# Value product of a hybrid attention step: P tiles stationary and 129 columns of V streamed, output turned once per head pair, five low parts on GpSimd

## The chip, the cores and the metric

The kernel runs on one core of one Trainium2 chip. The metric is the device time of one launch in microseconds. TensorE (PE) does the matrix products, VectorE (DVE), ScalarE (ACT) and GpSimd (POOL) the elementwise work, SyncE (SP) issues the DMAs. PEld is TensorE's weight load, which runs beside PE.

## The reference

Four layers run one after the other over 1024 latent and 256 context tokens (1280 queries) of width 1024. Their mixers are multi-head latent attention (MLA, layers 0 and 3), grouped-query attention (GQA, layer 1) and banded attention with a sink logit (SWA, layer 2). Each has 16 heads with values 64 wide. Latent queries see 512 cached and all 1024 latent keys (in SWA only those within 128 tokens), context queries see the 256 context keys. The part that the change touches is, per head:

```python
s = jnp.einsum('bqhgd,bkhd->bhgqk', qb, k) * scale
p = jax.nn.softmax(s, axis=-1)                     # SWA: one more column, the sink
o = jnp.einsum('bhgqk,bkhd->bqhgd', p, v)
out = (o.reshape(B, T, BRANCH) * jax.nn.silu(gate)) @ w_out
```

## The kernel before

Every f32 operand of a product is split into two f16 parts, high and low, and a product is the sum of high·high, high·low and low·high. `attention` handles one layer. It takes the heads in pairs (`NB` = 8 pairs, `body(i, first, last)`); each head is cut into steps. A step is a pair of key blocks of 128 against 512 queries (1024 score columns): 13 steps a head in MLA and GQA (queries 0 to 511, 512 to 1023, and one step for the 256 context queries), 9 in SWA. The three groups of queries are called units 0, 1 and 2. In the MLA layers the pairs between the first and the last run in a hardware loop; the other two layers are written out.

In step p the engines do this, in program order on each queue:

- PE (L2184) computes transposed scores (keys x queries) of step p into one of two score banks, then one or two "max entries" of the next head (L1931, scores again with the queries on the partitions, of which only the row maximum is used), then the value product of step p-2 (L2151, L2153, L2155), then the rest of the entries. A "turn" entry (L1961) transposes the negated row maxima, which ACT then writes as one more row of Q, so that the exponent comes out shifted.
- ACT computes the exponential twice, once as f32 (`p_f`, L2238) and once as f16 (`p_hi`, L2242).
- DVE subtracts them into `p_lo` (L2305), except in the steps of the list `pooled` (5, 7, 10), which POOL does (L2371). DVE also reduces the max entries (L1992).

The value product has V as the stationary operand: 64 value columns beside 64 columns of ones (so that rows 64 to 127 of the result are the softmax denominator), and P streams 512 columns at a time, in three products: `V` with `p_hi`, `VL` with `p_hi`, `V` with `p_lo`. The result is already transposed (values x queries). Its two banks `OB` are used in turn. At the end of a unit ACT makes the reciprocal of the denominator as Ln and Exp of 64 rows (L2258, L2260), DVE multiplies (L2285, `o_f`), POOL multiplies with the gate and splits the result into `H` (L2353, L2357, L2359), 64 rows at a time. In SWA the sink is added to the denominator by one more product (L2158) over three rows of Q.

`make_values` lays out V ahead of the first pair, and the entries share two banks `MB`. What sets the order is this program order and the semaphores alone; there is no scheduler.

Of the kernel before, what the change touches and what calls it, by code (L numbers as in the profile page):

```python
# [23 lines left out]
ALU = mybir.AluOpType  # L24
# [62 lines left out]
class Program:  # L87
    def __init__(self, nc, I, O):
# [10 lines left out]
        self.blk = sb("block_ones", [P, P], F32)  # L99
        self.c16 = sb("const_f16", [P, 5, P], F16)  # L100
# [75 lines left out]
    def start(self, nxt, CK, cache):  # L176
# [31 lines left out]
        consts = [(self.par[:], I["par"]), (cf[:], I["cf"]), (self.ones[:], I["ones"]), (self.blk[:], I["blk"])]  # L208
# [1468 lines left out]
    def attention(self, kind, Q, K, ada_layer, nxt, make_values, v_home=None):  # L1677
# [9 lines left out]
        wide = 3 * P + KD * 32  # L1687
        if v_home is None:
            V = sb("v_hi_ones", [P, 2, NKT, P], F16)
            VL = sb("v_lo_zeros", [P, 2, NKT, P], F16)  # L1690
        else:
            flat = v_home[:].rearrange("p s k n -> p (s k n)")
            V, VL = [flat[:, n * 2 * NKT * P:(n + 1) * 2 * NKT * P].rearrange("p (b t c) -> p b t c", b=2, c=P)
                     for n in range(2)]
        mx = None if swa else sb("max_parts", [P, 2, 4, 3], F32)
        m4 = sb("max_rows", [P, 2, 4], F32)
        turned = 3 if swa else 1
        negm = sb("neg_max", [P, 2, 4, turned], F16)
# [6 lines left out]
        if swa:  # L1705
            sink = self.par[:, self.par.shape[1] - 16:]
            es32 = sb("exp_sink", [P, 2, 4], F32)
            sink_raw = sb("sink_raw", [P, HEADS], F32)

        ident, negi, mask_above, mask_below, sink_ones = [self.c16[:, j] for j in range(5)]  # L1710

        SB, MB, OB = [bank[0], bank[1]], [bank[2][:, 0], bank[2][:, 1]], [bank[3][:, 0], bank[3][:, 1]]
# [52 lines left out]
        if swa:  # L1765
            entries = c_ + a_[:3] + [("turn", 2)] + a_[3:] + b_[:3] + [("turn", 0)] + b_[3:]
        else:
            entries = c_ + a_[:lag] + [("turn", 2)] + a_[lag:] + b_[:lag] + [("turn", 0)] + b_[lag:]
        if ada:
            entries += [("ada",)]  # L1770
        entries += [("turn", 1)]
        NE = len(entries)
        NM = NE - 3 - ada
        nmax = [sum(e[0] == "max" for e in entries[:k]) for k in range(NE + 1)]
        nturn = [sum(e[0] == "turn" for e in entries[:k]) for k in range(NE + 1)]
        turn_order = {e[1]: nturn[k] for k, e in enumerate(entries) if e[0] == "turn"}
# [4 lines left out]
        at_step = {j: [] for j in range(NS)}  # L1781
# [852 lines left out]
```

## Time and profile before

| | |
|---|---|
| median of 3 runs | 4035.09 us (4031.42 to 4038.88) |
| profiled execution, span | 4035.9 us |
| PE busy | 3893.6 us, 96% of the span |
| DVE, ACT, POOL busy | 2665.9, 2332.7, 1132.1 us (66%, 58%, 28%) |
| first and last score product of MLA attention, layer 0 | 401.6 and 1047.6 us |
| the same, GQA attention, layer 1 | 1454.5 and 2032.9 us |
| the same, SWA attention, layer 2 | 2426.0 and 2825.3 us |
| the same, MLA attention, layer 3 | 3283.2 and 3912.4 us |

A busy engine is one with an instruction running. A row of the timeline gives the start, the duration, the engine and line, what is written from what, and how many instructions are merged. The duration of one matrix product contains the pipeline behind it, so that products overlap in the rows; what one costs in a dense stream is the distance from its start to the next start.

### The profile page before, as it was taken

Reading aid. Unit: us, or ns where it says so; the run is one execution under the profiler, and the core shown is the slowest. Engines: PE = TensorE matmul, PEld = TensorE weight load, DVE = VectorE, ACT = ScalarE, POOL = GpSimd, SP = SyncE. Lnnn points to the kernel's source line nnn. Section 1 sums busy time; section 2 is a strip of 40 time slices with the busy share of each in tenths; the row PEclk is TensorE's granted clock in tenths of the full one; section 3 lists DMA queues with packets and bytes.
Section 4 is the critical chain, followed back from the end, with each engine's and each line's share of the span. In section 5 each row is a group of like instructions: output and inputs, shape, how many; then the busy total and the mean of one; then the engine's idle time right before and its main releaser. Section 6 shows DMA issues by size and latency. Waiting matters only on the chain. (4 is left out here: it accounts for less than half of the span.)

```text
span 4035.9 us, 57984 instructions
## 1 busy us (share of the span) xinstructions
PE 3893.6 (96%) x20892; PEld 1931.6 (48%) x20892; DVE 2665.9 (66%) x3536; ACT 2332.7 (58%) x3099; POOL 1132.1 (28%) x831
## 2 busy tenths in 40 slices
PE   6999999999999999999999999999999999999998
PEld 3554444444455544444445554555455444444444
DVE  6345777777457478888845427888543568777754
ACT  4433777777444358787843217888333457777762
POOL 0000343434230024454521003444210014444442
PEclk8999999999999999999999999999999999999999
DMA  6237323232102342222111324332111652212111
GB/s 241 65 102 223 92 55 77 60 72 64 60 32 76 116 113 51 65 64 62 37 66 51 108 91 117 91 90 63 62 46 70 186 151 46 55 42 55 42 38 66
DMA packets 376225, 329.42 MB, mean 82 GB/s; under 512 B 247664, under 2 KB 295344, under 8 KB 374480
## 3 DMA queue, kind: packets, MB, share of 16 engines
q1 hardware_dynamic: 376016, 326.60, 29.0%
q8 instruction: 135, 2.21, 0.2%
q14 instruction: 74, 0.61, 0.0%
HBM read 235.30 MB, written 91.23 MB: 81 GB/s over the span
## 5 line engine op out<-in xcount | busy, mean ns | idle before, releaser
L796 PE MATMUL bank<-H_hilo,w_hilo 128*128 128x512 f16 (+1 forms) x5760 | 1046.1, 344 | 13.6 <-DVE w_hilo L1046 10.1
L2238 ACT ACTIVATE p_f<-bank 128x1024 f32<-128x1024 f32 (+2 forms) x768 | 742.1, 966 | 485.9 <-PE bank L2184 454.6
L2184 PE MATMUL bank<-q_slots,k_slots 96*128 96x512 f16 (+7 forms) x3968 | 939.8, 366 | 6.0 <-PEq L1197 3.6
L1992 DVE TENSOR_REDUCE max_parts<-bank 128x1 f32<-128x512 f32 (+1 forms) x1248 | 799.1, 663 | 206.0 <-PE bank L1931 199.7
L2305 DVE TENSOR_TENSOR p_lo<-p_f,p_hi 128x1024 f16<-128x1024 f32 (+2 forms) x624 | 750.9, 1206 | 156.2 <-ACT p_hi L2242 151.6
L796 PEld LDWEIGHTS bank<-H_hilo,w_hilo 128*128 128x128 f16 x5760 | 563.7, 98 | 495.8 <-DVE w_hilo L1046 11.1
L2242 ACT ACTIVATE p_hi<-bank 128x1024 f16<-128x1024 f32 (+2 forms) x768 | 739.1, 962 | 0.0
L2184 PEld LDWEIGHTS bank<-q_slots,k_slots 96*128 96x128 f16 (+2 forms) x3968 | 369.7, 98 | 396.8 <-issue 27.0
L1931 PE MATMUL bank<-k_slots,q_slots 96*128 96x512 f16 (+4 forms) x1392 | 474.6, 369 | 24.9 <-DVE max_parts L1992 20.8
L2371 POOL TENSOR_TENSOR p_lo<-p_f,p_hi 128x1024 f16<-128x1024 f32 x144 | 315.6, 2192 | 567.5 <-ACT p_hi L2242 544.1
L2353 POOL TENSOR_TENSOR o_gated<-o_f,gate_rows 64x512 f32<-64x512 f32 (+1 forms) x192 | 235.5, 1226 | 778.5 <-DVE o_f L2285 571.5
L1010 ACT ACTIVATE z_ring<-bank 128x512 f32<-128x512 f32 (+1 forms) x192 | 87.5, 528 | 430.7 <-PE bank L796 417.2
L2151 PE MATMUL bank<-p_hi,cq_hilo 128*128 128x512 f16 (+1 forms) x832 | 308.5, 371 | 2.4 <-DVE p_lo L2305 1.8
L2155 PE MATMUL bank<-p_lo,cq_hilo 128*128 128x512 f16 (+1 forms) x832 | 307.9, 370 | 0.0
L2153 PE MATMUL bank<-p_hi,cq_hilo 128*128 128x512 f16 (+1 forms) x832 | 307.7, 370 | 0.0
L2151 PE MATMUL bank<-p_hi,v_hi_ones 128*128 128x512 f16 (+2 forms) x736 | 256.2, 350 | 21.9 <-DVE o_f L2285 14.9
L2153 PE MATMUL bank<-p_hi,v_lo_zeros 128*128 128x512 f16 (+2 forms) x736 | 257.3, 350 | 0.0
L2155 PE MATMUL bank<-p_lo,v_hi_ones 128*128 128x512 f16 (+2 forms) x736 | 255.8, 350 | 0.0
L1931 PEld LDWEIGHTS bank<-k_slots,q_slots 96*128 96x128 f16 (+1 forms) x1392 | 136.4, 98 | 231.2 <-DVE max_parts L1992 84.4
L1046 DVE SCALAR_TENSOR_TENSOR w_hilo<-w_f,w_hilo 128x1024 f16<-128x1024 f32 x56 | 68.6, 1224 | 258.8 <-ACT w_hilo L965 258.3
L2359 POOL TENSOR_TENSOR H_hilo<-o_gated,H_hilo 64x512 f16<-64x512 f32 (+3 forms) x192 | 218.0, 1136 | 22.9 <-POOL H_hilo L2357 13.3
L2357 POOL CAST H_hilo<-o_gated 64x512 f16<-64x512 f32 (+3 forms) x192 | 218.8, 1140 | 20.0 <-POOL o_gated L2353 12.3
(203 smaller groups left out, 3963.1 us busy)
## 6 DMA issues: line engine op xcount, KB each, us to landing
ada_w<-in_w_ada SPq DMA_DIRECT2D x48, 768.0 KB, 5.4
gate<-z_ring SPq DMA_DIRECT2D x32, 640.0 KB, 3.3
gate_rows<-gate SPq DMA_DIRECT2D x64, 320.0 KB, 4.0
q_slots<-q_mla SPq DMA_DIRECT2D x64, 240.0 KB, 3.2
k_mla<-H_hilo SPq DMA_DIRECT2D x64, 224.0 KB, 3.2
k_slots<-k_mla SPq DMA_DIRECT2D x64, 224.0 KB, 4.4
cq_hilo<-v_scratch SPq DMA_DIRECT2D x64, 224.0 KB, 3.3
w_f<-in_mla_in SPq DMA_DIRECT2D x24, 512.0 KB, 4.0
```

The source lines that it names most:

```text
L796: ins = pe.matmul(dst, lhs(a, k), rhs(b, k), start=(k == 0 and n == 0), stop=(k == nk - 1 and n == 2))
L1931: ins = pe.matmul(mb[:, 0:n], Q[0:kk, q_slot(hd, b), 0, q0:q0 + P], K[0:kk, k_slot(hd, b), 0, k0:k0 + n], start=True, stop=True)
L1992: dve.tensor_reduce(mx[:, par, t, c:c + 1], MB[(b * NE + k) % 2][:, 0:n], AX.X, ALU.max).then_inc(s_red.h, 1)
L2151: pe.matmul(d, V[:, b, kt], ph[:, slot[q], sel], start=first and n == 0, stop=False, skip_group_check=True)
L2153: pe.matmul(d, VL[:, b, kt], ph[:, slot[q], sel], start=False, stop=False, skip_group_check=True)
L2155: ins = pe.matmul(d, V[:, b, kt], pl[:, slot[q], sel], start=False, stop=fin, skip_group_check=True)
L2184: ins = pe.matmul(dst, lhs, rhs, start=(m == 0), stop=(m == len(ops) - 1), skip_group_check=swa)
L2238: act.activation(p32[:, p % 2, 0:cols], src, ACT.Exp, scale=scale).then_inc(s_p32.h, 1)
L2242: act.activation(ph[:, slot[p], 0:cols], src, ACT.Exp, scale=scale).then_inc(s_ph.h, 1)
L2305: dve.tensor_tensor(pl[:, slot[q], 0:cols], p32[:, q % 2, 0:cols], ph[:, slot[q], 0:cols], ALU.subtract).then_inc(s_pl.h, 1)
L2353: pool.tensor_tensor(og[rows, 0:nq], o32[rows, s, 0:nq], G[rows, q0:q0 + nq], ALU.mult).then_inc(s_og.h, 1)
L2371: pool.tensor_tensor(pl[:, slot[p], 0:cols], p32[:, p % 2, 0:cols], ph[:, slot[p], 0:cols], ALU.subtract).then_inc(s_pp.h, 1)
```

## The change

The value product is turned round. P is the stationary operand, one tile of 128 keys x 128 queries at a time, and V streams 129 columns: 64 low, 64 high and one of ones. Each tile of P takes two products, `p_hi` and `p_lo`, both against all 129 columns. The result has the queries on the partitions: four query tiles of 129 columns, two in each of the two banks of `OB`, so that a unit takes both banks. ACT copies it out (L2327), DVE takes the reciprocal of 128 x 4 denominators (L2357), POOL adds the low half to the high half and multiplies (L2411, L2416) into `o_n`, both heads of a pair side by side. Once per pair and unit PE turns `o_n` back with f32 transposes (L1951, new "out" entries in the rings of the max entries), DVE multiplies with the gate (L1961), POOL splits 128 rows at a time (L1969, L1971). The transposes of the row maxima take a 128-wide stationary operand, where only the first column is used. The sink product is gone; DVE adds the sink's exponential to the denominator. `pooled` becomes 3, 5, 7, 9, 11 (in MLA and GQA; SWA still has none). The gate is loaded once per pair in place of once per head.

```diff
-            V = sb("v_hi_ones", [P, 2, NKT, P], F16)
-            VL = sb("v_lo_zeros", [P, 2, NKT, P], F16)
+            V = sb("v_lo_hi_one", [P, 2, NKT, VC + 1], F16)
...
-        negm = sb("neg_max", [P, 2, 4, turned], F16)
+        negm = sb("neg_max", [P, 2, P + 4], F16)
...
+        out_step = [{8 if swa else 10: 0}, {3: 1, 4: 2}]
...
-        pooled = [] if swa else [5, 7, 10]
+        pooled = [] if swa else [3, 5, 7, 9, 11]
...
+        def turn_out(pe, mb, pair, u):
+            q0, nq = units[u]
+            pe.wait_ge(s_on.h, s_on.base + pair * 6 + u + 4)
+            for t in range(nq // P):
+                ins = pe.transpose(mb[:, t * P:(t + 1) * P], o_n[:, q0 // P + t], self.eye[:])
+            ins.then_inc(s_tr.h, 1)
+        def gate_out(dve, mb, pair, u):
+            q0, nq = units[u]
+            dve.wait_ge(s_tr.h, s_tr.base + pair * 3 + u + 1)
...
+            dve.tensor_tensor(og[:, q0:q0 + nq], mb[:, 0:nq], G[:, q0:q0 + nq], ALU.mult).then_inc(s_og.h, 1)
+        def split_out(pool, pair, u):
...
+            pool.tensor_copy(H(0), og[:, q0:q0 + nq]).then_inc(s_oh.h, 1)
+            pool.wait_ge(s_oh.h, s_oh.base + n)
+            pool.tensor_tensor(H(1), og[:, q0:q0 + nq], H(0), ALU.subtract).then_inc(s_ol.h, 1)
...
-                    ins = pe.transpose(r[0:turned, t * P:(t + 1) * P], negm[:, par, t], ident)
+                    ins = pe.transpose(r[:, t * P:(t + 1) * P], negm[:, par, t:t + P], ident)
...
-                        if above_zero(i * 6 + un - 1):
-                            pe.wait_ge(s_o.h, s_o.base + i * 6 + un - 1)
-                    for n, (kt, q0, nq, off, _) in enumerate(blocks):
...
-                        pe.matmul(d, V[:, b, kt], ph[:, slot[q], sel], start=first and n == 0, stop=False,
-                        pe.matmul(d, VL[:, b, kt], ph[:, slot[q], sel], start=False, stop=False,
-                        ins = pe.matmul(d, V[:, b, kt], pl[:, slot[q], sel], start=False, stop=fin,
-                    if swa and last:
-                        ins = pe.matmul(dst[:, 0:units[u][1]], sink_ones[mrow:mrow + turned],
+                    if first and above_zero(i * 6 + un):
+                        pe.wait_ge(s_ev.h, s_ev.base + i * 6 + un)
+                    fresh = [first, first]
+                    for half in range(2):
+                        for kt, q0, nq, off, _ in blocks:
+                            for j in range(nq // P):
...
+                                o = OB[:, half, t % 2 * VC:t % 2 * VC + VC]
+                                pe.matmul(o, ph[:, slot[q], sel], V[:, b, kt, 0:VC], start=fresh[half], stop=False,
+                                ins = pe.matmul(o, pl[:, slot[q], sel], V[:, b, kt, 0:VC], start=False,
...
-                            act.activation(r, OB[un % 2][HD:P, 0:nq], ACT.Ln).then_inc(s_lnd.h, 1)
-                            act.activation(r, r, ACT.Exp, scale=-1.0).then_inc(s_rd.h, 1)
+                            act.activation(o_raw[:, un % 2, 0:2 * nh].rearrange("p (h t) c -> p h (t c)", h=nh),
+                                           OB[:, 0:nh, 0:2 * VC], ACT.Copy).then_inc(s_ev.h, 1)
...
-                    dve.tensor_tensor(o32[rows, un % 2, 0:nq], OB[un % 2][0:HD, 0:nq], rden[rows, un % 2, 0:nq],
+                    dve.reciprocal(rd[:, un % 2, 0:nt], den).then_inc(s_rd.h, 1)
```

PE's queue in one step of the MLA loop, before: six score products, one max entry, six value products of 512 columns (`cq_hilo` is where V lies in this layer), the turn of two row-maximum tiles.

```order
L2184 MATMUL bank<-q_slots,k_slots 128x512 x6
L1931 MATMUL bank<-k_slots,q_slots 128x512
L2151 MATMUL bank<-p_hi,cq_hilo 128x512
L2153 MATMUL bank<-p_hi,cq_hilo 128x512
L2155 MATMUL bank<-p_lo,cq_hilo 128x512
...
L1961 MATMUL bank<-const_f,neg_max 1x128 x2
L1931 MATMUL bank<-k_slots,q_slots 128x512
```

The same place of the changed kernel. The two value rows stand eight times in a step, in alternation.

```order
L2247 MATMUL bank<-q_slots,k_slots 128x512 x6
L1993 MATMUL bank<-k_slots,q_slots 128x512
L2216 MATMUL bank<-cq_hilo,p_hi 128x129
L2219 MATMUL bank<-cq_hilo,p_lo 128x129
...
L2022 MATMUL bank<-const_f,neg_max 128x128 x2
L1993 MATMUL bank<-k_slots,q_slots 128x512
...
L1951 MATMUL bank<-identity,ckv_hilo 128x128 x4
```

Six products of 512 columns became sixteen of 129, and f32 transposes (L1951) stand among the entries: four, four and two of them at three steps of each pair of heads.

POOL's queue over most of one pair of heads in GQA, before: a `p_lo`, then the three operations of a unit on 64 rows.

```order
L2371 TENSOR_TENSOR p_lo<-p_f_7,p_hi 128x1024 x2
L2353 TENSOR_TENSOR o_gated<-o_f_7,gate_rows 64x512
L2357 CAST H_hilo<-o_gated 64x512
L2359 TENSOR_TENSOR H_hilo<-o_gated,H_hilo 64x512
L2371 TENSOR_TENSOR p_lo<-p_f_7,p_hi 128x1024
```

The same queue in the changed kernel.

```order
L2427 TENSOR_TENSOR p_lo<-p_f_7,p_hi 128x1024 x3
L2411 TENSOR_TENSOR o_lo_hi_den<-o_lo_hi_den 128x4x64
L2416 TENSOR_TENSOR o_normed<-o_lo_hi_den,recip_den 128x4x64
L2427 TENSOR_TENSOR p_lo<-p_f_7,p_hi 128x1024 x2
L1969 CAST H_hilo<-o_gated 128x512
L1971 TENSOR_TENSOR H_hilo<-o_gated,H_hilo 128x512
```

Two more low parts a head stand on POOL; its work at the end of a unit is now two operations of 256 elements a row per head, and the split once per pair.

## Rows read from the trace of the kernel before

**Rows 1.** The page, part 1: busy us, share of the span, instructions
```profile
PE 3893.6 (96%) x20892; PEld 1931.6 (48%) x20892; DVE 2665.9 (66%) x3536; ACT 2332.7 (58%) x3099; POOL 1132.1 (28%) x831
```

**Rows 2.** Busy time by stretch: MLA, GQA, SWA attention; then PEclk, DMA share, GB/s
```profile
500.00:1000.00 500.00, 497.83 (x2485) 224.22 (x2483) 381.66 (x565) 354.67 (x428) 201.64 (x146) 1.00 0.28 68
1500.00:2000.00 500.00, 483.88 (x2403) 213.91 (x2402) 432.43 (x631) 397.45 (x479) 246.23 (x167) 1.00 0.24 59
2500.00:2800.00 300.00, 290.50 (x2037) 161.79 (x2036) 259.81 (x336) 244.06 (x396) 125.49 (x108) 1.00 0.35 86
```

**Rows 3.** The page, part 5: one of the three lines of the value product
```profile
L2151 PE MATMUL bank<-p_hi,cq_hilo 128*128 128x512 f16 (+1 forms) x832 | 308.5, 371 | 2.4 <-DVE p_lo L2305 1.8
L2151 PE MATMUL bank<-p_hi,v_hi_ones 128*128 128x512 f16 (+2 forms) x736 | 256.2, 350 | 21.9 <-DVE o_f L2285 14.9
```

**Rows 4.** Timeline, MLA: one step at a unit's end
```profile
592.53 0.38 PE L2151 MATMUL bank<-p_hi,cq_hilo 128*128 128x512 f16 x1
...
593.51 1.02 ACT L2242 ACTIVATE p_hi<-bank 128x1024 f16<-128x1024 f32 x1
...
593.61 0.38 PE L2155 MATMUL bank<-p_lo,cq_hilo 128*128 128x512 f16 x1
...
595.78 0.38 PE L2151 MATMUL bank<-p_hi,cq_hilo 128*128 128x512 f16 x1
```

**Rows 5.** Timeline, SWA: value products with 128 moving columns
```profile
2605.71 0.22 PE L2151 MATMUL bank<-p_hi,v_hi_ones 128*128 128x128 f16 x1
2605.72 0.10 PEld L2153 LDWEIGHTS bank<-p_hi,v_lo_zeros 128*128 128x128 f16 x1
2605.77 0.22 PE L2153 MATMUL bank<-p_hi,v_lo_zeros 128*128 128x128 f16 x1
...
2605.88 0.33 PE L2151 MATMUL bank<-p_hi,v_hi_ones 128*128 128x384 f16 x1
```

**Rows 6.** Timeline, SWA: the sink product between a 256-column product and scores
```profile
2610.76 0.27 PE L2155 MATMUL bank<-p_lo,v_hi_ones 128*128 128x256 f16 x1
...
2610.97 0.28 PE L2158 MATMUL bank<-q_slots,const_f 3*128 3x256 f16 x1
...
2611.18 0.50 PE L2184 MATMUL bank<-q_slots,k_slots 128*128 128x384 f16 x2
```

**Rows 7.** Timeline, MLA: a turn of four row-maximum tiles
```profile
597.08 0.38 PE L1931 MATMUL bank<-k_slots,q_slots 96*128 96x512 f16 x1
597.39 0.20 PEld L1961 LDWEIGHTS bank<-const_f,neg_max 128*1 128x1 f16 x4 [0.42 <-issue]
597.39 0.38 PE L1961 MATMUL bank<-const_f,neg_max 128*1 128x128 f16 x4
...
597.71 1.47 PE L2184 MATMUL bank<-q_slots,k_slots 96*128 96x512 f16 x6
```

**Rows 8.** Timeline, projection: f32 products, 2560 columns in six records
```profile
129.25 2.31 PE L1142 MATMUL bank<-squares,ones 128*128 128x512 f32 x6
131.40 26.12 PE L796 MATMUL bank<-H_hilo,w_hilo 128*128 128x512 f16 x144
```

**Rows 9.** GQA attention alone (1455 to 2033): groups by line and shape
```profile
L2305 DVE TENSOR_TENSOR p_lo<-p_f,p_hi 128x1024 f16<-128x1024 f32 x143 | 179.7, 1257 | 11.5 <-ACT p_hi L2242 10.8
...
L2285 DVE TENSOR_TENSOR o_f<-bank,recip_den 64x512 f32<-64x512 f32 x31 | 21.1, 682 | 2.8 <-ACT recip_den L2260 2.2
...
L2305 DVE TENSOR_TENSOR p_lo<-p_f,p_hi 128x512 f16<-128x512 f32 x15 | 10.2, 682 | 0.0
...
L1996 DVE TENSOR_REDUCE max_rows<-max_parts 128x4 f32<-128x12 f32 x30 | 5.0, 166 | 1.0
...
L2258 ACT ACTIVATE recip_den<-bank 64x512 f32<-64x512 f32 x31 | 18.4, 593 | 0.8
...
L2371 POOL TENSOR_TENSOR p_lo<-p_f,p_hi 128x1024 f16<-128x1024 f32 x48 | 106.5, 2219 | 134.6 <-ACT p_hi L2242 121.9 <-issue 12.6
```

**Rows 10.** Timeline, SWA: a GpSimd operation and a low part on VectorE
```profile
2619.28 0.68 POOL L2359 TENSOR_TENSOR H_hilo<-o_gated,H_hilo 64x256 f16<-64x256 f32 x1
2619.34 1.17 DVE L2305 TENSOR_TENSOR p_lo<-p_f,p_hi 128x512 f16<-128x512 f32 x1
```

More of the change, by code:

```diff
@@ new lines, in split_out, with emit_entry @@
+        def split_out(pool, pair, u):
+            q0, nq = units[u]
+            n = pair * 3 + u + 1
+            H = lambda c: self.H[:, c, at(pair), q0:q0 + nq].rearrange("p a n -> p (a n)")
+            pool.wait_ge(s_og.h, s_og.base + n)
+            pool.tensor_copy(H(0), og[:, q0:q0 + nq]).then_inc(s_oh.h, 1)
+            pool.wait_ge(s_oh.h, s_oh.base + n)
+            pool.tensor_tensor(H(1), og[:, q0:q0 + nq], H(0), ALU.subtract).then_inc(s_ol.h, 1)
+        def emit_entry(pe, pair, b, k):
+            mb = entry_bank(b, k)
+            hd = pair * 2 + b
+            e = entries[b][k]
+            if e[0] == "out" and not above_zero(pair):
+                return
+            if not (swa and e[0] == "turn"):
+                wait_bank(pe, pair, b, k)
@@ L1939, in emit_entry @@
                 if b == 0:
-                    if not above_zero(hd):
+                    if not above_zero(pair):
                         return
-                    ada_turn(pe, mb, hd // 2)
+                    ada_turn(pe, mb, pair)
                     return
@@ L2080, in _ @@
             def _(sp):
[L2081 removed]
+                load_gate(sp, 0)
                 load_ada(sp, 0, 0)
@@ L2105, in body @@
                         load_v(sp, h + 1, kv, 1 - j)
[L2107 to L2109 removed]
                         load_ada(sp, i + j, 1 - j)
+                        if j == 0 and not first:
+                            sp.wait_ge(s_og.h, s_og.base + i * 3)
+                            load_gate(sp, i)
                 pairs_of_heads(sp, body)
@@ L2147, in pv @@
-                    for n, (kt, q0, nq, off, _) in enumerate(blocks):
-                        d = dst[:, q0 - units[u][0]:q0 - units[u][0] + nq]
-                        sel = slice(off, off + nq)
-                        fin = last and n == len(blocks) - 1 and not swa
-                        pe.matmul(d, V[:, b, kt], ph[:, slot[q], sel], start=first and n == 0, stop=False,
-                                  skip_group_check=True)
-                        pe.matmul(d, VL[:, b, kt], ph[:, slot[q], sel], start=False, stop=False,
-                                  skip_group_check=True)
-                        ins = pe.matmul(d, V[:, b, kt], pl[:, slot[q], sel], start=False, stop=fin,
-                                        skip_group_check=True)
@@ L2169, in body @@
                             g = i * P2 + p
+                            nb, npair = 1 - b, i + b
+                            todo = at_step[nb][p % NS]
+                            if last and b == 1:
+                                todo = []
                             if p % NS == first_of[u]:
@@ L2266, in _, with inverse @@
             def _(dve):
-                def normed(i, p):
+                def inverse(i, p, first):
                     e = p - 3
-                    if e < 0 and i_first[0]:
+                    if e < 0 and first:
                         return
@@ L2306, in body @@
                                               ALU.subtract).then_inc(s_pl.h, 1)
-                        if not mla:
-                            normed(i, p)
+                        inverse(i, p, first)
                         for k in found[early[p % NS]:]:
-                            take_entry(dve, i * 2 + b + 1, 1 - b, k)
-                        if mla:
-                            normed(i, p)
+                            take_entry(dve, i + b, 1 - b, k)
+                        if last and NS <= p < P2 and p % NS in out_step[0]:
+                            gate_out(dve, MB[0], NB - 1, 0)
                     if first:
```

436 lines of the change are left out of this document (234 added, 202 removed).

## The prediction

> **What bounds the kernel now.** First the page: PE is busy for 3893.6 of 4035.9 us [rows 1]. A busy share can hide slack, so next the stretches. In MLA attention PE is busy 497.8 of 500 us at full clock, in GQA 483.9 of 500, in SWA 290.5 of 300; DVE is second with 76%, 86% and 87%, ACT has 71%, 79% and 81% [rows 2]. So PE is the bound in all four attention phases (646, 578, 399 and 629 us by the table, 2252 us together, with 32 MLA, 16 GQA and 16 SWA heads), and microseconds taken from PE there come off the time until the next engine is reached. In GQA and SWA that engine is near. The phases between (projections) are not touched. The value product waits for almost nothing: 2.4 us idle before its MLA line, 21.9 us before the other, mostly for `o_f`, the operation that frees an `OB` bank [rows 3].
>
> **What the value product costs, and its change.** Starts six products apart in a step give the pitch of a 512-column product: from 592.53 to 593.61 are five of them, 0.216 us each [rows 4]. That is 512 columns at 2.4 GHz plus some 2.5 ns. The code gives the columns: a head has 12 key blocks against 1024 queries and 2 against 256 in MLA and GQA, 12,800 columns for each of the three lines, and 7,424 in SWA; over 48 and 16 heads 733,184. At 2.4 GHz these are 305.5 us a line, 916.5 for three; with 2.5 ns for each of the 3 x (832 + 736) products [rows 3] it is 928 us.
>
> After it there are 733,184 / 128 = 5728 tiles of P with two products of 129 columns, 11,456 in all. The nearest row is a value product with 128 moving columns and its own 128x128 weights: from 2605.71 to 2605.88 three start, 0.057 us apart, though each weight load takes 0.10 us [rows 5]. The second load began while the first of the three products did, so loads overlap the product before and each other. I take 129 columns at 2.4 GHz and 2.5 ns, 0.0563 us: 645 us. Term one: **-283 us**. Its lower bound in speed is the load itself, 0.10 us if bursts of sixteen behave worse than bursts of three (a rival below).
>
> **Sink product.** The 256-column product starts at 2610.76 and the scores behind the sink product at 2611.18, 0.42 us where 0.11 would do: 0.31 us, of which 0.11 is the stream and 0.2 are gaps around it [rows 6]. With 512 columns it is some 0.41. 32 of these and 16 of those: **-18 us**.
>
> **Turns.** The product ahead of a turn starts at 597.08 and the turn at 597.39, 0.09 us late; the four small transposes take until 597.71 where 4 x 0.057 would do, again 0.09; the weight load of one column was not made early, PEld idles 0.42 us before it [rows 7]. With 128 stationary columns the load has the shape of all the others, which run ahead [rows 5]. 3 turns x 64 heads x 0.185 us = **-35 us**; the bound is nothing, if the gap belongs to transposes as such. I take the full value, since the sink product, which is no transpose and has only three rows, has the same gaps [rows 6].
>
> **Output transposes.** 10 a pair, 32 pairs: 320 f32 transposes of 128 columns. The trace has no f32 transpose. An f32 product leaves two records, and six records with 2560 columns take 2.15 us, 0.84 ns a column and record [rows 8]; so 0.215 us for a whole f32 product of 128 columns, 0.107 for one record. An f16 transpose costs 0.057 or so a piece inside its gaps [rows 7]. Bounds 18 and 69 us; I take one f32 record each, between them: **+34 us**.
>
> PE's own sum is -283 - 18 - 35 + 34 = -302 us, some 5 us a MLA head and 4 a SWA head (SWA has 0.58 of the value columns).
>
> **What the other engines then cost.** *The output bank.* A unit now takes both banks of `OB`, so the first value product of a unit waits for ACT's copy of the last one. In MLA the six value products end issuing at 593.61 + 0.22, while ACT runs `p_hi` until 594.53; a copy of 516 columns takes about what Ln takes on 512, 0.59 us [rows 4, 9], so the bank is free at 595.1. The next value product was due at 595.78 [rows 4], and is due 0.4 us earlier when the six become sixteen of 0.0563 (0.90 for 1.30 us): a margin of about 0.2 us, sometimes missed. I take 0.1 us for each of three units, 0.3 us a head, 10 us for 32 heads. *GQA.* A head takes 36.1 us. DVE has 86.5% of it, 31.2 us. It loses two low parts of 1.26 us, and `o_f` (21.1 us over 16 heads for the large form, 0.4 us a head for the small one, 1.7 in all); it gains half a gate product on 128 rows a head (0.68 x 2 + 0.4 over two heads, 0.9) and three reciprocals of four columns, at 0.17 as the small reduction, 0.5 [rows 9]. That leaves 28.4 us. PE's busy 34.9 us fall by 5 to 30. With 95% of PE's load on DVE, in steps where DVE's part is uneven (steps 0, 1, 2 have a low part each, while steps 3, 5, 7 have none), PE will wait more than its 3% of now: I take 1.2 us a head more, as much again as its present idle time, 19 us. *SWA.* No low part moves. DVE has 21.6 us of 24.9 a head, loses `o_f` and a small subtraction (2.1) and gains 0.9 for the gate and six small operations (1.0): 21.4. PE falls from 24.1 to 20.1. DVE becomes the bound here, and at the 96% at which PE runs now the head takes 22.3 us, 1.5 more than PE and its present idle time would give: 24 us. ACT loses Ln and Exp and gains a copy, POOL gains 2 x 2.2 us a head and drops the 64-row operations (18 us a head before, about 17 after, of 32): neither bounds.
>
> POOL's low part takes 2.22 us against 1.26 [rows 9]; it is due two steps after its exponential starts, 4.8 us in GQA, of which ACT takes 2.05: hidden, by 0.5 us. If POOL is late by a split (two operations), the value product of the next odd step is late by the same; that is in the 1.2 us. The gate's load moved behind a wait for the previous pair's last gate product (step 4); behind it in SP's queue stand only loads for the next head, eight steps later, and it is needed at step 10 of the second head: nothing. The projection's start waits for two last splits, 2.3 us, beside 24 products of 0.216: nothing.
>
> **Sum.** -302 + 10 + 19 + 24 = -249 us against the profiled span of 4035.9, which is the median (4035.1) within 1 us: **3787 us**.
>
> **The rivals.**
> *Another engine becomes the bound all along.* In SWA a low part of 512 columns took 1.17 us while a GpSimd operation ran beside it for 0.62 of them, against 0.68 alone [rows 9, 10]: the two exclude each other. Five low parts a head on POOL and 2.2 us each make more such meetings. The Trainium skill, "SBUF — State Buffer", section "Who interferes with whom", says that a VectorE instruction with two SBUF inputs contends with a GpSimd instruction that reads SBUF, by an exclusive lock; by that rule, the trace agrees. For it: GQA and SWA have DVE at 87% today. Against: POOL's total hardly grows, and every low part moved leaves DVE. If a meeting costs 1 us a head in MLA, 3 in GQA and 2 in SWA, it is 3787 + 32 + 48 + 32 = 3899.
> *The weight load sets the pitch (slower).* The change doubles the loads of the attention and halves the stream that covers each. If in a burst of sixteen a product cannot follow faster than one load, 0.10 us [rows 5], the value product takes 1146 us, 218 more than now; with -19 us of the other PE terms and nothing lost to other engines the time is 4235. It decides from a pitch of 0.083 us, where PE's sum is nothing. Against: the pitch of 0.057 in the row. The Trainium skill, "TensorE: Matmul & The Clock Gate", section "Back-to-back issue gap", gives about 81 ns for a sustained stream of loads and 128-column products, and 56 ns only for the product by itself; by that the product would take 928 us, and the kernel about 4017. By that rule the trace does not agree, as far as bursts of three show it.
> *The single output bank.* If ACT comes one step late, its copy stands behind two more exponentials, 2.05 us, and PE waits at every unit: at 1 us for each of 192 units the time is 3979; it ends on the slower side from 1.3 us a unit. Against: ACT is busy for 71 to 81% today, and loses work [rows 2].
> *Nothing new idles.* DVE's relief lets PE run dense in MLA and GQA: 3787 - 53 = 3734, with cheap transposes 3718.
>
> **How the numbers follow.** Chances: forecast (3735 to 3845) 0.64; engines bound (3845 to 3930) 0.20; no idle 0.07; output bank 0.04; weight load 0.05. Range 3715 to 3890: below it almost nothing, above it the tail of the engine case (0.06), the bank and the load. Keeping the turn gaps (+35) and whole f32 products (+35) both fit in it. A measurement tells 0.2% from no change; faster 0.95, same 0.01, slower 0.04.
>
> **What the changed profile would show.** Pitch of L2216 and L2219 at 0.056 (0.08 or 0.10 if a load binds). Turn rows start 0.216 after a 512-column product. PE in MLA above 98%, in GQA 92 to 95%, in SWA 90%. First value product of a unit waiting for L2327 some 0.1 us, no more. L1951 groups of four at 0.4 to 0.9 us. The prediction falls with PE idle above 10% in MLA, or low parts on DVE with a mean above 1.5 us.

## The result and the profile after

The changed kernel takes 3928.15 us (median of 4 runs, 3924.41 to 3931.06) against 4036.55 of the kernel before on the same chip: ratio 0.9731, 95% interval 0.9718 to 0.9745. That is 108 us less, where 249 were forecast; the time lies 38 us above the range. The profiled span is 3924.1 us, 111.8 less than before.

The page, part 1, of the changed kernel, beside [rows 1]:

```profile
PE 3638.0 (93%) x27916; PEld 2180.3 (56%) x27916; DVE 2497.6 (64%) x3536; ACT 2192.9 (56%) x2859; POOL 1076.9 (27%) x931
```

PE's busy time fell by 255.6 us, so its idle time rose from 142 to 286: more than half of what PE gained is given back as waiting. Where, the stretches show. The first three answer to [rows 2], the last is layer 3; columns as there:

```profile
500.00:1000.00 500.00, 473.97 (x4328) 300.26 (x4327) 353.85 (x578) 355.45 (x421) 228.71 (x182) 1.00 0.29 66
1500.00:2000.00 500.00, 463.82 (x4319) 293.30 (x4320) 386.80 (x608) 377.14 (x447) 241.74 (x198) 0.99 0.26 66
2400.00:2700.00 300.00, 261.91 (x2810) 188.41 (x2809) 250.09 (x366) 215.96 (x332) 79.28 (x112) 1.00 0.39 91
3300.00:3700.00 400.00, 364.55 (x3263) 229.33 (x3262) 286.69 (x456) 277.61 (x330) 177.69 (x144) 1.00 0.26 52
```

PE is busy for 94.8% in the first MLA layer, 92.8% in GQA, 87.3% in SWA, 91.1% in the last MLA layer. From the first to the last score product of each attention phase:

| | before: length, PE idle | after: length, PE idle | after, PE busy less |
|---|---|---|---|
| MLA, layer 0 | 646.0, 4.5 | 607.6, 34.0 | 67.9 |
| GQA, layer 1 | 578.4, 18.0 | 535.0, 40.2 | 65.5 |
| SWA, layer 2 | 399.2, 13.8 | 382.4, 49.2 | 52.2 |
| MLA, layer 3 | 629.2, 4.7 | 613.3, 52.4 | 63.6 |
| sum | 2252.8, 41.0 | 2138.3, 175.8 | 249.3 |

The value product itself did what was expected. Page, part 5, beside [rows 3]:

```profile
L2216 PE MATMUL bank<-cq_hilo,p_hi 128*128 128x129 f16 x3200 | 410.2, 221 | 25.2 <-ACT o_lo_hi_den L2327 15.4
...
L2216 PE MATMUL bank<-v_lo_hi_one,p_hi 128*128 128x129 f16 x2528 | 326.2, 221 | 33.1 <-ACT o_lo_hi_den L2327 18.0
```

The 221 ns contain the pipeline; the pitch is in the timeline. First an MLA step of sixteen products, then a turn:

```profile
600.29 0.23 PE L2216 MATMUL bank<-cq_hilo,p_hi 128*128 128x129 f16 x1
600.36 0.22 PE L2219 MATMUL bank<-cq_hilo,p_lo 128*128 128x129 f16 x1
...
601.15 0.22 PE L2219 MATMUL bank<-cq_hilo,p_lo 128*128 128x129 f16 x1
...
609.69 0.22 PE L2219 MATMUL bank<-cq_hilo,p_lo 128*128 128x129 f16 x1
609.75 0.28 PE L2022 MATMUL bank<-const_f,neg_max 128*128 128x128 f16 x2
609.86 0.38 PE L1993 MATMUL bank<-k_slots,q_slots 96*128 96x512 f16 x1
```

Fifteen pitches in 0.86 us are 0.057 each, with a load of 0.10 us for every one, and two turns take 0.11 with no gap at either side, where [rows 7] has 0.09 on each. It holds beyond this burst: of the 11,456 value products in the trace 10,695 are followed by another, 0.058 us later in the mean. What is new are these waits of PE (us in all, times, longest), between the first and the last score product of layers 0 to 3 in turn:

```profile
PE bank L1951 <- DVE max_parts L2062: 17.1, 21, 1.3
PE bank L2216 <- ACT o_lo_hi_den L2327: 6.4, 18, 0.4
PE bank L1993 <- DMA k_slots<-kpe_mla: 6.3, 7, 2.3
...
PE bank L1993 <- DVE max_parts L2062: 25.2, 61, 3.1
...
PE bank L1951 <- DVE max_rows L2054: 17.6, 14, 1.3
PE bank L2216 <- ACT o_lo_hi_den L2327: 13.8, 17, 1.3
...
PE bank L1951 <- DVE max_parts L2062: 17.8, 21, 1.3
PE bank L2022 <- DVE neg_max L2067: 17.3, 15, 1.2
```

Three kinds stand out. **The output entry.** L1951 is the last of the entries of its step, and waits for the ring's bank. Timeline of layer 3, where the entries ahead of it are two row-maximum products (L1993) and their reductions on DVE are L2062:

```profile
3347.91 1.22 DVE L2374 TENSOR_TENSOR p_lo<-p_f,p_hi 128x1024 f16<-128x1024 f32 x1
...
3348.01 0.60 PE L1993 MATMUL bank<-k_slots,q_slots 96*128 96x512 f16 x2
...
3349.04 1.28 DVE L2062 TENSOR_REDUCE max_parts<-bank 128x1 f32<-128x512 f32 x2
...
3349.86 0.65 PE L1951 MATMUL bank<-identity,ckv_hilo 128*128 128x128 f32 x4 [1.26 <-DVE max_parts L2062]
...
3350.35 0.38 PE L2247 MATMUL bank<-q_slots,k_slots 96*128 96x512 f16 x1
```

The two entries ahead of it filled both banks at 3348.01 while DVE had just begun a low part; its reductions came after, and PE stood for 1.26 us. The four transposes take 0.49 us to the next start, 0.1225 each in the mean: by their starts 0.16 behind the first and 0.11 behind each of the others.

**The held small operation.** POOL's low part of step 11 against DVE's negated maximum, layer 3:

```profile
3413.54 2.12 POOL L2427 TENSOR_TENSOR p_lo<-p_f,p_hi 128x1024 f16<-128x1024 f32 x1 [4.86 <-ACT p_hi L2313]
3414.33 1.37 DVE L2067 TENSOR_SCALAR neg_max<-max_rows 128x4 f16<-128x4 f32 x1
...
3415.75 0.23 PE L2022 MATMUL bank<-const_f,neg_max 128*128 128x128 f16 x1 [1.12 <-DVE neg_max L2067]
```

An operation on four columns starts inside POOL's and ends with it; its median over the kernel is 0.171 us. PE's turn waits for it, and everything queued behind the turn.

**The output bank.** ACT's copy (L2327) against the first value product of the next unit, layer 3:

```profile
3340.64 1.02 ACT L2313 ACTIVATE p_hi<-bank 128x1024 f16<-128x1024 f32 x1
3341.55 0.61 ACT L2327 ACTIVATE o_lo_hi_den<-bank 128x516 f32<-128x516 f32 x1
...
3342.21 0.23 PE L2216 MATMUL bank<-cq_hilo,p_hi 128*128 128x129 f16 x1 [0.40 <-ACT o_lo_hi_den L2327]
```

The kernel before had a wait at this place too, for `o_f`. In GQA and SWA together it was nearly as long as the new one (3.5 and 13.8 us); in MLA the new one is all addition. Kernel before, GQA, then SWA:

```profile
PE bank L2151 <- DVE o_f L2285: 9.6, 14, 0.8
...
PE bank L2151 <- DVE o_f L2285: 5.3, 13, 0.5
```

### The profile page after: what moved, and what is told of

It is laid out like the page before. It is cut to its first block and busy times, and to the rows that moved or that the text cites. A ratio compares the mean times of both kernels' runs of the same rounds, so it can differ in the third digit from the quotient of the medians.

```text
span 3924.1 us, 71972 instructions
## 1 busy us (share of the span) xinstructions
PE 3638.0 (93%) x27916; PEld 2180.3 (56%) x27916; DVE 2497.6 (64%) x3536; ACT 2192.9 (56%) x2859; POOL 1076.9 (27%) x931
## 5 line engine op out<-in xcount | busy, mean ns | idle before, releaser
L2062 DVE TENSOR_REDUCE max_parts<-bank 128x1 f32<-128x512 f32 (+1 forms) x1248 | 797.2, 663 | 273.0 <-PE bank L1993 271.8
L2427 POOL TENSOR_TENSOR p_lo<-p_f,p_hi 128x1024 f16<-128x1024 f32 x240 | 531.1, 2213 | 683.2 <-ACT p_hi L2313 683.2
L2374 DVE TENSOR_TENSOR p_lo<-p_f,p_hi 128x1024 f16<-128x1024 f32 (+1 forms) x528 | 606.8, 1150 | 158.2 <-ACT p_hi L2313 151.7
L1993 PE MATMUL bank<-k_slots,q_slots 96*128 96x512 f16 (+4 forms) x1392 | 471.9, 368 | 52.6 <-DVE max_parts L2062 44.7
L2216 PE MATMUL bank<-cq_hilo,p_hi 128*128 128x129 f16 x3200 | 410.2, 221 | 25.2 <-ACT o_lo_hi_den L2327 15.4
L2219 PE MATMUL bank<-cq_hilo,p_lo 128*128 128x129 f16 x3200 | 408.7, 219 | 0.0
L2216 PE MATMUL bank<-v_lo_hi_one,p_hi 128*128 128x129 f16 x2528 | 326.2, 221 | 33.1 <-ACT o_lo_hi_den L2327 18.0
L2216 PEld LDWEIGHTS bank<-cq_hilo,p_hi 128*128 128x128 f16 x3200 | 308.0, 97 | 85.1 <-ACT o_lo_hi_den L2327 29.3
L2219 PEld LDWEIGHTS bank<-cq_hilo,p_lo 128*128 128x128 f16 x3200 | 312.7, 98 | 31.4
L2219 PE MATMUL bank<-v_lo_hi_one,p_lo 128*128 128x129 f16 x2528 | 325.8, 220 | 0.0
L2216 PEld LDWEIGHTS bank<-v_lo_hi_one,p_hi 128*128 128x128 f16 x2528 | 243.6, 97 | 79.0 <-DVE p_lo L2374 48.4
L2219 PEld LDWEIGHTS bank<-v_lo_hi_one,p_lo 128*128 128x128 f16 x2528 | 246.8, 98 | 18.5 <-issue 0.6
L1993 PEld LDWEIGHTS bank<-k_slots,q_slots 96*128 96x128 f16 (+1 forms) x1392 | 132.0, 97 | 186.7 <-DVE max_parts L2062 115.8
L2411 POOL TENSOR_TENSOR o_lo_hi_den<-o_lo_hi_den 128x256 f32<-128x256 f32 (+1 forms) x192 | 144.4, 752 | 263.1 <-ACT o_lo_hi_den L2327 260.7
```

What stands on the lines that cost most here:

```text
L1993: ins = pe.matmul(mb[:, 0:n], Q[0:kk, q_slot(hd, b), 0, q0:q0 + P], K[0:kk, k_slot(hd, b), 0, k0:k0 + n], start=True, stop=True)
L2062: dve.tensor_reduce(mx[:, par, t, c:c + 1], entry_bank(b, k)[:, 0:n], AX.X, ALU.max).then_inc(s_red.h, 1)
L2216: pe.matmul(o, ph[:, slot[q], sel], V[:, b, kt, 0:VC], start=fresh[half], stop=False, skip_group_check=True)
L2219: ins = pe.matmul(o, pl[:, slot[q], sel], V[:, b, kt, 0:VC], start=False, stop=True, skip_group_check=True)
L2374: dve.tensor_tensor(pl[:, slot[q], 0:cols], p32[:, q % 2, 0:cols], ph[:, slot[q], 0:cols], ALU.subtract).then_inc(s_pl.h, 1)
L2411: pool.tensor_tensor(hi, hi, lo, ALU.add).then_inc(s_sum.h, 1)
```

## The experiments

The theory: PE's own sum was nearly right, and the term for the other engines was three times too small, because of these waits. The rivals: PE's sum itself is wrong; or another engine is the bound all along, so that only the mass of DVE's and POOL's work counts and no single place. Twelve kernels ran, all from the changed one unless said. Time is the median, and each ratio is to the kernel before on the same chip.

| | us | against changed | ratio to before, 95% |
|---|---|---|---|
| changed | 3928.15 | | 0.9731 (0.9718 to 0.9745) |
| output entry first in its step | 3905.70 | -22 | 0.9672 (0.9656 to 0.9689) |
| three low parts on POOL | 3936.06 | +8 | 0.9753 (0.9736 to 0.9769) |
| copy between the exponentials | 3926.64 | -2 | 0.9730 (0.9713 to 0.9746) |
| kernel before, five on POOL | 4068.85 | | 1.0079 (1.0063 to 1.0096) |
| four low parts on POOL | 3905.64 | -23 | 0.9674 (0.9660 to 0.9689) |
| half of every low part | 3846.32 | -82 | 0.9523 (0.9508 to 0.9537) |
| half on POOL only | 3893.47 | -35 | 0.9646 (0.9633 to 0.9660) |
| half on DVE only | 3873.59 | -55 | 0.9596 (0.9583 to 0.9609) |
| narrow turns | 3942.09 | +14 | 0.9767 (0.9753 to 0.9781) |
| three mends | 3882.65 | -46 | 0.9615 (0.9602 to 0.9628) |
| mends, four on POOL | 3868.15 | -60 | 0.9588 (0.9575 to 0.9602) |
| the same, an eighth of every low part | 3799.81 | -128 | 0.9410 (0.9395 to 0.9426) |

**The output entry first**, ahead of the value product, on PE's queue and on DVE's.

```diff
-                made = [base[k] for k in base_step[j]] + ([("out", out_step[b][j])] if j in out_step[b] else [])
+                made = ([("out", out_step[b][j])] if j in out_step[b] else []) + [base[k] for k in base_step[j]]
...
-                            for k in todo[:early[p % NS]]:
+                            for k in todo[:early_of(nb, p % NS)]:
```

> The changed kernel, but an out entry stands first in its step, ahead of the value product, on TensorE and on VectorE; nothing else differs. Theory 1 (order): the out entry is the fourth entry of its step and needs a bank that VectorE reads only behind a low part; in the changed kernel that is 56.5 us of idle TensorE before the f32 transposes (L1951), and about 10 us more hidden in the modelled ends. Moved, most of it goes: 3875 to 3895 us. Theory 2 (load): VectorE is simply too busy, and the wait moves to the next entry: 3915 to 3935 us.

Measured: 22 us less, between the ranges of the two theories. The wait before the output entry is gone in MLA (layer 0 -10.6 us, layer 3 -12.7). In GQA the phase grew by 6, and the wait ahead of the other entries from 25.2 to 30.7. Waits in layer 3:

```profile
PE bank L2023 <- DVE neg_max L2068: 17.3, 15, 1.2
PE bank L1994 <- DVE max_parts L2063: 7.8, 24, 0.5
PE bank L2217 <- ACT o_lo_hi_den L2328: 7.5, 17, 1.5
```

So the place among the entries is worth 23 of the 35 us that were listed for it in MLA, and the turn's wait, 17.3 us in both, is another matter.

**Three low parts on POOL.**

```diff
-        pooled = [] if swa else [3, 5, 7, 9, 11]
+        pooled = [] if swa else [5, 7, 10]
```

> The changed kernel with three low parts on GpSimd (steps 5, 7, 10) as before, nothing else undone. Theory A (exclusion of VectorE and GpSimd): the low part of step 11 on GpSimd holds up the small negated-maximum operation of step 12 on VectorE, which the turn waits for (17 us idle TensorE in layer 3); without it that wait goes, and the kernel takes 3900 to 3920 us. Theory B (load): VectorE has two low parts of 1.2 us more in each of 48 heads, and the queue of maxima falls behind in GQA: 3940 to 3970 us.

Measured: 8 us more, with an interval that overlaps the changed kernel's, and between the ranges of the two theories. In layer 0 it is +18, everywhere else nothing or less. With more low parts on DVE the output entry waits longer for its bank, in layer 0 and in layer 3:

```profile
PE bank L1951 <- DVE max_parts L2062: 29.5, 21, 1.8
...
PE bank L1951 <- DVE max_parts L2062: 30.6, 21, 2.0
```

In layer 3 the turn's wait is gone, as the theory of exclusion says, and the 13 us more at the output entry eat it up; in layer 0 there was no such wait to win.

The list is thus a trade between DVE ahead of the output entry and POOL beside small operations.

**The copy between ACT's exponentials.**

```diff
                             act.activation(p32[:, p % 2, 0:cols], src, ACT.Exp, scale=scale).then_inc(s_p32.h, 1)
+                            copy_out(i, p, first)
...
-                            act.activation(o_raw[:, un % 2, 0:2 * nh].rearrange("p (h t) c -> p h (t c)", h=nh),
```

> The changed kernel with ScalarE's copy of the output bank between its two exponentials in place of behind them, so the bank is free about 1 us earlier and the f16 exponential comes 0.6 us later in three of 13 steps. Theory 1 (the single output bank costs): the 33 us in which TensorE waits for that copy, and some 10 us behind it, go: 3890 to 3905 us. Theory 2 (ScalarE is as critical in those steps): what is won is lost on the low part behind the later exponential: 3920 to 3935 us.

Measured: 2 us less, which the intervals don't tell from nothing, and in the range of the second theory. SWA gained 6.5 us. Layer 0 lost 5, and there a wait for a DMA rose from 6.3 to 14.7: what the copy alone did in that layer is not shown. Waits in SWA:

```profile
PE bank L1951 <- DVE max_rows L2054: 17.6, 14, 1.3
PE bank L2216 <- DVE p_lo L2379: 9.6, 32, 0.5
PE bank L1989 <- DVE max_rows L2054: 9.1, 35, 0.4
```

The copy's wait is gone, but half of it stands again, 3 us each before the low part, which comes later when `p_hi` does, and before the entries. The 33 us that the page lists at the output bank (15.4 and 18.0) were not 33 us to be had.

**Five low parts on POOL in the kernel before.** The same edit of the list as in the change, alone.

> The kernel before with five low parts on GpSimd, nothing else. Theory A (exclusion): the wait for the negated maximum appears here too, about 1 us in each head of layer 3, and some in GQA: 4045 to 4060 us. Theory B (load): VectorE is relieved, TensorE's few waits for it in GQA go, TensorE is bound: 4025 to 4036 us.

Measured: 32.6 us slower (4068.85 against 4036.27), 0.8%, and 9 us above the range of exclusion. The theory of load, with its 4025 to 4036, is out. The longer stretches are GQA (+11.6) and layer 3 (+16.5). Waits in GQA, then in layer 3:

```profile
PE bank L2151 <- POOL p_lo L2371: 12.2, 16, 1.6
...
PE bank L1961 <- DVE neg_max L1999: 9.4, 15, 0.8
```

The negated maxima of four columns in layer 3 take 854 ns in the mean there, 169 in the kernel before. In GQA it is the low part on POOL itself that comes late, where the prediction had it hidden, by 0.5 us; in the changed kernel it is 1.4 us. So this part of the change is no relief by itself: where PE has no time to give back, it costs.

**Four low parts on POOL**, the list without step 11.

> The changed kernel with the low part of step 11 back on VectorE (steps 3, 5, 7, 9 on GpSimd). Exclusion: in layer 3 the 17 us of waiting for the negated maximum (and 2.5 us behind it) go, in GQA some of the same, against 1.2 us more VectorE work a head: layer 3 12 to 20 us shorter, the whole 3905 to 3920 us. Load: layer 3 no shorter, the whole 3928 to 3945 us.

Measured: 23 us less, 11 of them in layer 3, where the turn's wait left the list, and 4 in the other three attention phases; the rest isn't in them. That is the range of exclusion, though layer 3 gave 1 us less than it asks. The group of the operation in layer 3, changed kernel first, then this one (times, busy us and mean ns):

```profile
L2067 DVE TENSOR_SCALAR neg_max<-max_rows 128x4 f16<-128x4 f32 x31 | 23.5, 757 | 1.1
```

```profile
L2067 DVE TENSOR_SCALAR neg_max<-max_rows 128x4 f16<-128x4 f32 x30 | 5.1, 170 | 1.0
```

One POOL operation less lengthens DVE's work (2530.9 us against 2497.6) and still wins: the place counted, not the mass. In layer 0, whose turns stand at other steps, the same group took 170 ns in the changed kernel already, and that phase stayed at 607.5 us.

**Half of the low parts.** A low part is subtracted for the first half of its columns only, so half of the low product is left out; on both engines, on POOL only, on DVE only. By the code the four buffers of `p_lo` are shared by both engines, so the rest of a halved part is zero only until a wider part has stood there; PE's products are the same either way.

```diff
-                            dve.tensor_tensor(pl[:, slot[q], 0:cols], p32[:, q % 2, 0:cols], ph[:, slot[q], 0:cols],
+                            dve.tensor_tensor(pl[:, slot[q], 0:cols // 2], p32[:, q % 2, 0:cols // 2], ph[:, slot[q], 0:cols // 2],
```

> The changed kernel with every low part, on VectorE and GpSimd, computed for only the first half of its columns (the other half of the low part is zero, so a part of the result's low-order correction is left out). TensorE and ScalarE do the same work. VectorE has 0.55 us less in each step. If the queue on VectorE is what TensorE waits for, most of the 95 us listed as waits for VectorE go: 3840 to 3870 us. If the single output bank and TensorE's own order hold it back: 3900 us or more.

> The low parts on GpSimd alone are cut to half of their columns (the other half of each stays zero, so part of the low product is left out); those on VectorE are whole. Half low parts on both engines gave 3846, 82 us under the changed kernel. If what PE pays for is mostly the exclusion between the two engines, this alone brings more than half of the 82 us: 3870 to 3885. If it is VectorE's own load and order, it brings little: 3905 to 3925.

> The low parts on VectorE alone are cut to half of their columns (the rest stays zero, left out of the low product), those on GpSimd are whole. If VectorE's own load and the order on its queue are what PE pays for, above all in GQA and SWA (where GpSimd has none), this alone brings most of the 82 us that both halves brought: 3850 to 3875. If it is the exclusion, a low part on GpSimd still holds the small operations back and it brings 20 to 35 us: 3893 to 3908.

Measured: -82, -35 and -55 us: nearly a sum (89), with DVE the larger part. By phase, layers 0 to 3: POOL's half brings 0, 13, -1 and 14 us, DVE's 5, 21, 17 and 11. POOL's low parts cost in GQA and by the held operation in layer 3, and shortening DVE's does nothing for that hold. In layer 3, POOL's half first, DVE's half second:

```profile
PE bank L2022 <- DVE neg_max L2067: 2.3, 12, 0.2
```

```profile
PE bank L2022 <- DVE neg_max L2067: 21.7, 15, 1.5
```

Both halves together ended inside the case of DVE's queue, POOL's half between its two cases and DVE's inside its first, near the edge: the 82 us are not one cause. That PE follows the load of DVE shows most in GQA and SWA (21 and 17 us).

**Narrow turns**, the old form of the turn in the changed kernel.

```diff
-                    ins = pe.transpose(r[:, t * P:(t + 1) * P], negm[:, par, t:t + P], ident)
+                    ins = pe.transpose(r[0:1, t * P:(t + 1) * P], negm[:, par, t:t + 1], ident)
```

> The changed kernel with the old form of the turns: a stationary operand of one column in place of 128, all else as changed. The prediction gave the wide form -35 us. If the gap ahead of a one-column product (about 0.09 us over a plain product, one for each of the 384 to 640 such products, or one per group of two to four) is real and PE still sets the time in MLA, the kernel becomes 20 to 40 us slower than the changed one, 3950 to 3965, and turn rows again show 0.30 to 0.32 us from the product before. If, now that PE waits for 5 to 13% of the attention phases, the gaps fall into waits that were there anyway, the loss is under 10 us (3928 to 3938).

Measured: 14 us more, between the two cases. The gaps are back:

```profile
611.16 0.22 PE L2219 MATMUL bank<-cq_hilo,p_lo 128*128 128x129 f16 x1
611.31 0.27 PE L2022 MATMUL bank<-const_f,neg_max 128*1 128x128 f16 x2
611.51 0.39 PE L1993 MATMUL bank<-k_slots,q_slots 96*128 96x512 f16 x1
```

From 611.16 to the turn are 0.15 us where 0.06 stood at full width, and the two turns take 0.20 for 0.11. The page counts such a gap as busy: PE's busy time is 3673.5 us, 35.5 more, which is the -35 of the prediction, while PE's idle time fell by 16. The other way round, the wide turn alone in the kernel before, has no time: with the wider tile of row maxima the kernel's tiles no longer fit in SBUF.

**The mends together**: the output entry first in MLA only, the copy between the exponentials in SWA only, four low parts on POOL in layer 3 only; then four in GQA and layer 0 too.

```diff
-        pooled = [] if swa else [3, 5, 7, 9, 11] if ada else [3, 5, 7, 9]
+        pooled = [] if swa else [3, 5, 7, 9]
```

> The changed kernel with three mends: out entries first in their step in the MLA layers only (22 us), the output copy between the exponentials in SWA only (6.5 us there), and four low parts on GpSimd in layer 3 only (15 us). If they are independent: 3880 to 3890 us.

> The three mends (output entry first in its step in MLA, the copy between the exponentials in SWA) with four low parts on GpSimd (steps 3, 5, 7, 9) in all of MLA and GQA, where the version with three mends had four in the last layer only. If the low part of step 11 on GpSimd costs PE time in layer 0 and GQA as it does in the last layer, the kernel gains 3 to 10 us over 3882.7. If layer 0 has room on GpSimd and VectorE is the tighter one there, since the output entries then stand right behind a low part, it is level or up to 8 us slower (3880 to 3891).

Measured: 3882.65, in its range: the three together bring 46 us, and apart they were put at 44. Then 3868.15 us, 14 us less again, more than expected. By the profiles 4 us of it are in layer 0, 3 in GQA and 1 each in SWA and layer 3; the rest isn't in the attention phases. This version is 60 us faster than the changed kernel and 4.1% faster than the kernel before, and computes all of the reference. Layer 3 in it, beside the last row of the windows above:

```profile
3300.00:3700.00 400.00, 385.70 (x3442) 242.30 (x3440) 302.53 (x493) 291.50 (x346) 166.67 (x143) 1.00 0.27 55
```

PE is busy for 96.4% in place of 91.1%.

**The floor of PE.** The last version with an eighth of every low part (the rest left out, as above), PE's queue unchanged.

> The version with the mends and four low parts on GpSimd, and of every low part only the first eighth of its columns is subtracted, on both engines (the rest stays zero and so is left out of the low product; PE's own queue is as it was). This takes VectorE and GpSimd out of PE's way as far as the low parts hold them. If the prediction's sum for PE alone was right (-302 us, with what was measured since: -297) and the loss sits in what the other engines cost, the kernel comes to 3755 to 3800: 4036 less 297, and 15 to 60 us for the output bank, the output entries and the DMA waits that stay. If PE's own sum was too large (products or transposes that cost more in a full stream than in the bursts read), it stays above 3810 even with these engines free.

Measured: 3799.81 us, the upper end of the case that PE's sum is right. The page, part 1, and PE's waits in GQA:

```profile
PE 3604.3 (95%) x27916; PEld 2188.1 (58%) x27916; DVE 2055.7 (54%) x3584; ACT 2190.9 (58%) x2859; POOL 602.7 (16%) x887
```

```profile
PE bank L2219 <- ACT o_lo_hi_den L2311: 16.1, 37, 1.0
PE bank L1954 <- DVE max_parts L2065: 4.0, 7, 0.6
```

PE has as many products as in the changed kernel (27916), but is busy for 33.7 us less. The end of a product, of which a row shows some 0.16 us beyond the pitch (0.22 for 0.057), counts as busy ahead of a wait, so fewer waits leave less of it. It is the number of waits and not their length: in the attention phases PE stands still 388 times in the changed kernel, 380 times in the last full version (busy for 3638.2 us, no less than the changed one, though its idle time is 58 us less) and 223 times here. In the four attention phases PE's busy time is 1930.9 us, 280.9 less than before, and the listed idle 90.5, of which the output bank has 16 in GQA, where it had 3.5 in the changed kernel: with DVE out of the way the next wait in line comes out. Another is the DMA of `k_slots` in MLA, 18 us here and 6 in the changed kernel. In SWA 16.6 us before the output entry stay even here, so low parts aren't their cause; by the code each entry of that layer waits for the one before it, since a row maximum takes both banks.

## Why the prediction was right in sign and wrong in size

**Right: the bound, the value product, the sink, the turns.** PE was the bound, and a pitch of 0.0563 us holds over bursts of sixteen with a load before each, so the term of -283 stands and the rival of the weight load falls: its own condition, 0.083 us, isn't met. The Trainium skill, "TensorE: Matmul & The Clock Gate", section "Back-to-back issue gap", gives about 81 ns for such a stream; the traces disagree, 57 ns over sixteen. The turns gave -35 in PE's busy time, but only 14 of them are time of this kernel, as part of the gaps would fall into waits. The sink product is gone; its -18 was not tried alone.

**Nearly right: the output transposes.** 0.11 us from start to start for 0.107, but 0.05 more at the first of each group: 0.1225 in the mean, so +39 for +34, and PE's sum is -297 for -302. Taking one f32 record each was a choice between bounds of 18 and 69 us, so that it came out near is in part luck. The floor run bears the sum out from below: -281 busy with waits left that still hide some of it.

The starts in the two traces say the same without a model of the ends. If every product in the four phases costs its dense pitch (0.216 us for 512 columns, 0.0563 for 129, 0.1225 for a transpose), they come to 2062.8 us before and 1809.7 after, 253 less (some 50 us of other f32 products stand apart on both sides): the -283, the +39 and 9 us for the sink product's own stream. What the distances from start to start hold beyond that grew from 138 to 277 us, though the 45 us of gaps around turns and sink products went: 183 us more.

**Wrong: the part "What the other engines then cost".** It put 53 us there (10 for the bank in MLA, 19 in GQA, 24 in SWA). The attention phases show 135 us more listed idle. The difference between PE's sum and what its busy time shows (297 less 249) is 48 more: mostly ends of products ahead of waits, that the page counts as busy; 32 of them went away with the waits in the floor run. That makes 183 for 53, 130 of the miss of 141; 5 more are in the transposes, and 6 lie within what runs and phases differ by. Layer by layer the sum forecast 74, 60, 40 and 74 us less, and 38, 43, 17 and 16 were measured. By its own steps:

- *MLA, 0.3 us a head.* The largest miss: the two layers got 77 us more listed idle, where 10 were given, and ended 94 us behind their forecast. The sum priced the transposes as PE time only, and never asked where the entry stands. As the last of its step it needs a bank that DVE frees only after a low part: 35 us of listed waits in MLA, and moving it to the front brought 23 back there. The working named whom PE waits for at the end of a unit, but not at the new entry.
- *"The two exclude each other".* The meeting was seen and priced by its mean, 1 us a head, in a rival. What cost most was one place: POOL's step 11 over the negated maximum that layer 3's turn waits for, 757 ns for 170, 17 us of waits; dropping that low part brought 11 us there. That the hold follows POOL's instruction shows in POOL's half (292 ns in the mean) too. The prediction looked for meetings of POOL with DVE's low parts, but those of 1024 columns got no longer in MLA and GQA (1.22 to 1.23 us in the mean, 1.26 to 1.32 before); the one that hurt is with the smallest operation on DVE. The Trainium skill, "SBUF — State Buffer", section "Who interferes with whom", names tensor_scalar, which this one is, among those that can take the pair of ports that GpSimd needs, and says that whoever comes first keeps it for a whole instruction; by that rule, the trace agrees: 1.37 us for 0.17, ending with POOL's.
- *The single output bank.* In MLA 14 us are listed for the 10 that were given, so the term was right. The 17 in GQA and SWA take the place of 15 that the kernel before had for `o_f`, 6 less in GQA and 8 more in SWA, where moving the copy won 6.5 back. Taking the wait away brought nothing outside SWA; in GQA the waits for low parts rose by 4 us in its place, in MLA it is not shown what did.
- *GQA and SWA.* GQA's 92.8% is inside the 92 to 95 that were named, SWA's 87.3 is below the 90. The price was 19 and 24 us; listed idle rose by 22 and 35. In SWA DVE was to become the bound at 96%; it is busy for 83%, while PE waits 17.6 us at the output entry, which had no price.
- *"Every low part moved leaves DVE".* Taken as a relief; in the kernel before it costs 33 us, and four beat both three and five in the changed one.

Neither sign that was to topple the prediction came (PE idle above 10% in MLA, low parts above 1.5 us): PE is idle for 9% in layer 3 and low parts take 1.2 us, so the signs were set too wide. Of the rivals, the engines as bound (3899, chance 0.20) came nearest. But its mechanism, a little at every meeting, is only part of it: two operations moved and one entry of a list dropped gave 60 us back with all the work still done, while 28% less work on POOL in layer 0 brought nothing and 14% less on DVE there 5. The load itself is the rest: with low parts nearly gone another 68 us came off.

**Open.** Why the output entry first costs 6 us in GQA, and where the last two full versions differ outside the attention phases, wasn't settled; nor was a free bank for the output entries in SWA tried. The half and eighth runs leave work out, so the 68 us show what the low parts cost PE and not what a kernel that does all the work can win.

## What to carry to other kernels

When a change adds an instruction to a queue, price its wait as well as its work: name the bank it needs, who frees it and what stands ahead of that on the other queue. When work moves to GpSimd, look at which small VectorE operation on the path of the bound engine runs beside it, since it can be held until the GpSimd instruction ends. And as a bound engine gets faster, its waits add up only in part: moving the copy that 33 us were listed for brought 2, moving the entry that 35 were listed for brought 23.

## What the runs showed of the hardware that was not expected

- A weight load of 128 x 128 that takes 0.10 us stays hidden at a pitch of 0.057 us over sixteen products, while one of one column costs a gap of 0.09 us ahead of its product and another behind (35 us of PE's busy time over the kernel, 14 us of its time here).
- An f32 transpose of 128 x 128 has one record and follows the one before it after 0.11 us; behind the first of a group it is 0.16, so that a group of four takes 0.49 us.
- A VectorE operation of 4 columns that normally takes 0.17 us took 1.37 us beside a GpSimd one of 2.12 us, and 1.04 us in the mean over layer 3 where only VectorE's low parts were halved.
- PE's busy time is not a fixed cost of its instructions: with the same 27916 products it was 3638.0 us with 388 stretches of idle time in the attention phases, 3638.2 with 380, and 3604.3 with 223.
